# Sums of a layer norm and of a doubly applied norm folded on VectorE, in a two-block transformer kernel

## What is computed

```python
def layernorm(x, g, b):
    mu = jnp.mean(xf, axis=-1, keepdims=True)
    var = jnp.mean(jnp.square(xf - mu), axis=-1, keepdims=True)
    y = (xf - mu) * lax.rsqrt(var + LN_EPS)
    return (y * g + b)

def conformer_conv(h, w_pw1, b_pw1, w_dw, b_dw, ln_g, ln_b, w_pw2, b_pw2):
    u = h @ w_pw1 + b_pw1
    a, gate = jnp.split(u, 2, axis=-1)
    u = a * jax.nn.sigmoid(gate)
    u = depthwise_causal_conv(u, w_dw) + b_dw            # 31 taps
    u = jax.nn.silu(layernorm(u, ln_g, ln_b))
    return u @ w_pw2 + b_pw2

# end of the first block and start of the second: x is normed twice in a row
x = x + sqrelu_mlp(h, ff_w1, ff_w2)                      # second layer: stages up1, down1
x = rmsnorm(x, final_norm_g)                             # out1
h = rmsnorm_2(x, norm_ff1_2)                             # ffa: feeds the gate/up product gu1
```

## Time and profile before

| | |
|---|---|
| median of 3 runs | 1479.2 us (1478.4 to 1481.55) |
| time of the profiled execution | 1481.04 us |
| its span (first to last instruction) | 1478.9 us |
| busy TensorE (PE) / VectorE (DVE) / ScalarE (ACT) | 98% / 74% / 46% of the span |
| granted TensorE clock, mean | 0.998 of full speed |
| LN beside memk1 and memv1, pw2 begins | 148 to 197.3 us |
| down1 | about 778 to 867 us |

### The profile page before, as it was taken

One profiled execution on the slowest core, in us unless ns is written; L12 is line 12 of the kernel. 1 busy time (PEld: TensorE's weight loads), 2 busy tenths in 40 slices (PEclk: granted clock), 3 DMA queues, 4 the chain that ended last, 5 costly groups with the idle time before them and its releaser, 6 DMA issues.

```text
span 1478.9 us, 21797 instructions
## 1 busy us (share of the span) xinstructions
PE 1446.7 (98%) x8556; PEld 1261.6 (85%) x8556; DVE 1092.1 (74%) x1638; ACT 682.5 (46%) x891; POOL 31.5 (2%) x20
## 2 busy tenths in 40 slices
PE   7999999999999999999999999999999999999997
PEld 6878888888889777888888998878888889888887
DVE  3799457688867756557887769998678768788654
ACT  2222254455434554545554345544454356555542
POOL 0000000000000000000000000000005200000000
PEclk9999999999999999999999999999999999999999
DMA  8544444355686433534557747767754445476452
GB/s 316 195 171 150 153 138 158 114 171 202 233 289 218 153 127 128 171 115 143 199 196 270 253 178 259 287 227 240 249 197 154 143 134 188 171 253 217 151 176 68
DMA packets 60192, 279.31 MB, mean 189 GB/s; under 512 B 6633, under 2 KB 8106, under 8 KB 35275
## 3 DMA queue, kind: packets, MB, share of 16 engines
q1 hardware_dynamic: 55672, 266.49, 52.0%
q10 hardware_dynamic: 4434, 11.64, 2.2%
HBM read 273.89 MB, written 4.19 MB: 188 GB/s over the span
## 4 chain that ended last, share of the span: by engine, by line
PE 84%; DVE 8%; DMA 5%; ACT 2%; issue 1%; DVEq 0%; SPq 0%; ACTq 0%
PE acc L474 33%; PE acc L476 17%; PE acc L495 10%; DMA ada_w<-in_ada 5%; PE acc L513 3%; PE acc L514 3%; PE acc L515 3%; DVE wsplit L1650 3%; PE acc L613 2%; PE stat L698 2%; DVE ada_w L2021 2%; PE stat L808 2%; PE score L770 2%; PE acc L617 1%; PE turned L716 1%
## 5 line engine op out<-in xcount | busy, mean ns | idle before, releaser
L474 PE MATMUL acc<-hA,wsplit 128*128 128x512 f32 x1664 | 590.6, 399 | 6.4 <-DVE tsum L1664 4.8
L476 PE MATMUL acc<-hA,wsplit 128*128 128x256 f32 x1664 | 463.9, 279 | 0.0
L1112 ACT ACTIVATE wsplit<-raw 128x2048 fp32r<-128x2048 f32 (+3 forms) x206 | 365.8, 1777 | 191.5 <-PE acc L476 147.0
L1650 DVE TENSOR_TENSOR wsplit<-raw,wsplit 128x2048 fp32r<-128x2048 f32 (+3 forms) x206 | 436.9, 2123 | 7.5 <-ACT wsplit L1112 7.4
L474 PEld LDWEIGHTS acc<-hA,wsplit 128*128 128x128 f32 x1664 | 312.3, 188 | 84.9 <-DVE tsum L1664 5.9
L476 PEld LDWEIGHTS acc<-hA,wsplit 128*128 128x128 f32 x1664 | 313.3, 188 | 0.4
L474 PE MATMUL acc<-hid,wsplit 128*128 128x512 f32 x648 | 225.5, 391 | 1.6 <-issue 1.6
L476 PE MATMUL acc<-hid,wsplit 128*128 128x256 f32 x648 | 182.7, 282 | 0.0
L1122 ACT ACTIVATE lowp<-acc 128x512 f32<-128x512 f32 (+1 forms) x118 | 69.0, 585 | 188.5 <-PE acc L476 164.4
L474 PEld LDWEIGHTS acc<-hid,wsplit 128*128 128x128 f32 x648 | 121.7, 188 | 27.5 <-issue 1.9
L476 PEld LDWEIGHTS acc<-hid,wsplit 128*128 128x128 f32 x648 | 122.5, 189 | 0.1
(11 more groups left out here) (294 smaller groups left out, 2083.7 us busy)
## 6 DMA issues: line engine op xcount, KB each, us to landing
raw<-in_gu SPq DMA_DIRECT2D x44, 1024.0 KB, 5.0
ada_w<-in_ada SPq DMA_DIRECT2D x144, 256.0 KB, 4.7
raw<-in_up SPq DMA_DIRECT2D x32, 1024.0 KB, 4.9
raw<-in_down SPq DMA_DIRECT2D x32, 1024.0 KB, 5.0
raw<-in_dn SPq DMA_DIRECT2D x32, 704.0 KB, 4.3
raw<-in_pw SPq DMA_DIRECT2D x8, 1024.0 KB, 6.4
raw<-in_memk SPq DMA_DIRECT2D x8, 1024.0 KB, 4.9
raw<-in_memv SPq DMA_DIRECT2D x8, 1024.0 KB, 5.3
```

Of the source, the lines that this page charges most:

```text
L474: nc.tensor.matmul(dst.rearrange("p (s t) -> p s t", s=2), w, h, start=start, stop=False, skip_group_check=True)
L476: return nc.tensor.matmul(dst[:, 0:T], lo_w, h[:, 0, :], start=False, stop=stop, skip_group_check=True)
L1112: nc.scalar.activation(wsplit[:, slot, 0, 0:elems_of(n)], raw[:, slot, 0:elems_of(n)], ACT.Copy).then_inc(S("w_hi"), 1)
L1650: V.tensor_tensor(wsplit[:, slot, 1, 0:e], src, wsplit[:, slot, 0, 0:e].bitcast(F32), ALU.subtract).then_inc(S("w_lo"), 1)
```

## The change

The eight tiles of the convolution and the eight tiles of squares of LN are each added up on VectorE to two tiles (three additions of 128x512 for the mean, three for the squares), and TensorE sums each result with two products in place of eight. All four squares are made after chunk 2 of memk1, the inverse root after chunk 3, and the activation goes in three parts behind chunks 0, 1 and 2 of memv1. `ffa` is added to FOLDED; since it has two sums, VectorE also multiplies the squares with their gains and adds them into `lowp` (`weigh`).

```diff
-FOLDED = ["fox", "mixn", "ffb", "final2"]
+FOLDED = ["fox", "ffa", "mixn", "ffb", "final2"]
+LN_MEAN, LN_SQUARES = 3, 6
@@ TensorE, norm_sums
-                            mm = nc.tensor.matmul(stat[:, 1, :], gain_sq[:, 2 * p + j, :], aux[:, p % 2, j, :],
+                            weights = ones[:] if p == first else gain_sq[:, 2 * p + j, :]
+                            squares = lowp[:, j, :] if p == first else aux[:, at, j, :]
+                            mm = nc.tensor.matmul(stat[:, 1, :], weights, squares,
@@ TensorE, LN
             def ln_mean():
                 stat_read(norm_index("mem") + 1)
-                for kt in range(KT):
-                    pe.wait_ge(S("conv_tile"), kt + 1)
-                    mm = nc.tensor.matmul(stat[:, 0, :], ones[:], conv[:, kt, :], start=kt == 0, stop=kt == KT - 1)
+                ln_sum(LN_MEAN)
+
+            def ln_sum(folds):
+                pe.wait_ge(S("ln_folded"), folds)
+                for j in range(2):
+                    mm = nc.tensor.matmul(stat[:, 0, :], ones[:], tsum[:, 0, j, :], start=j == 0, stop=j == 1)
                 mm.then_inc(S("ln_stat"), 1)
-            def ln_squares(pairs):      # eight products over four pairs: gone
...
-                   after=lambda c: ln_mean() if c == 2 else ln_squares([0, 1]) if c == 3 else None)
-            native("memv1", mem_h[1], after=lambda c: ln_squares([2, 3]) if c == 0 else None)
+                   after=lambda c: ln_mean() if c == 2 else ln_sum(LN_SQUARES) if c == 3 else None)
+            native("memv1", mem_h[1])
@@ ScalarE
                     if p >= 2:
-                        wait("ln_stat", p)
+                        wait("ln_folded", LN_MEAN + 1)
...
-                (0, 2): lambda: ln_squares([0, 1]),
-                (0, 3): lambda: ln_squares([2, 3]),
-                (1, 0): ln_root,
-                (1, 1): ln_silu,
-                (1, 2): lambda: None,
+                (0, 2): lambda: ln_squares(range(PAIRS)),
+                (0, 3): ln_root,
+                (1, 0): lambda: ln_silu([0, 1]),
+                (1, 1): lambda: ln_silu([2]),
+                (1, 2): lambda: ln_silu([3]),
@@ VectorE, stage down1
+                def weigh(p):
+                    wait("gain_sq", 2)
+                    for q in range(0 if p == 1 else p, p + 1):
+                        if q >= 1:
+                            wait("weighted", q)
+                        for j in range(2):
+                            squares, weight = aux[:, q % 2, j, :], gain_sq[:, 2 * q + j, 0:1]
+                            if q == 0:
+                                last = V.tensor_scalar(lowp[:, j, :], squares, weight, None, ALU.mult)
+                            else:
+                                last = V.scalar_tensor_tensor(out=lowp[:, j, :], in0=squares, scalar=weight,
+                                                              in1=lowp[:, j, :], op0=ALU.mult, op1=ALU.add)
+                        last.then_inc(S("weighted"), 1)
+                    wait("weighted", p + 1)
...
+                        if norm_name == "ffa":
+                            weigh(p)
                         V.tensor_tensor(aux[:, 1, :, :], aux[:, 1, :, :], aux[:, 0, :, :],
                                         ALU.add).then_inc(S("squares_folded"), 1)
@@ VectorE, LN
             conv_taps(KT * TAPS, KT)
+            def ln_fold(into, first, second, done):
+                V.tensor_tensor(tsum[:, into, :, :], first, second, ALU.add).then_inc(S("ln_folded"), 1)
+                wait("ln_folded", done)
+            wait("conv_tile", KT)
+            ln_fold(0, conv[:, 0:2, :], conv[:, 2:4, :], 1)
+            ln_fold(1, conv[:, 4:6, :], conv[:, 6:8, :], 2)
+            ln_fold(0, tsum[:, 0, :, :], tsum[:, 1, :, :], LN_MEAN)
             for n in range(AHEAD):
                 split_lo(STAGE["pw2"], n, n)
-            wait("conv_tile", KT)
             wait("ln_stat", 1)
...
                 V.tensor_tensor(c2, c2, spread(mu[:], 2), ALU.subtract).then_inc(S("ln_centred"), 1)
+            wait("ln_sq", 2)
+            ln_fold(0, aux[:, 0, :, :], aux[:, 1, :, :], LN_MEAN + 1)
+            wait("ln_sq", PAIRS)
+            ln_fold(1, aux[:, 0, :, :], aux[:, 1, :, :], LN_MEAN + 2)
+            ln_fold(0, tsum[:, 0, :, :], tsum[:, 1, :, :], LN_SQUARES)
             split_lo(STAGE["pw2"], AHEAD, AHEAD)
```

More of the change, by code:

```diff
@@ L688, in norm_sums @@
                         stat_read(q)
-                    if name == "ffa" and p == 0:
+                    if name == "ffa" and p == first:
                         pe.wait_ge(S("gain_sq"), 2)
@@ L864, in ln_mean @@
                 stat_read(norm_index("mem") + 1)
-                for kt in range(KT):
-                    pe.wait_ge(S("conv_tile"), kt + 1)
-                    mm = nc.tensor.matmul(stat[:, 0, :], ones[:], conv[:, kt, :], start=kt == 0, stop=kt == KT - 1)
-                mm.then_inc(S("ln_stat"), 1)
-            def ln_squares(pairs):
[L871 to L876, removed]
+                ln_sum(LN_MEAN)
[3 more added lines that the diff above has]
+                    mm = nc.tensor.matmul(stat[:, 0, :], ones[:], tsum[:, 0, j, :], start=j == 0, stop=j == 1)
+                mm.then_inc(S("ln_stat"), 1)
             native("memk0", mem_h[0], {kt: (S("mem_h"), kt + 1) for kt in range(KT)}, after=relative_biases)
@@ L1461, in ln_root @@
                 wait("log_table", LN_TABLE)
-                wait("ln_stat", 1 + PAIRS)
+                wait("ln_stat", 2)
                 inverse_root("ln_root", 0, stat[:, 0, :], rstd[:], 1 / D, col("ln_eps"))
@@ L1467, in ln_hi, with ln_silu @@
                 nc.scalar.activation(hM[:, 2 * p:2 * p + 2, 0:T], tsum[:, p % 2, :, :], ACT.Copy).then_inc(S("ln_hi"), 1)
-            def ln_silu():
-                for p in range(PAIRS):
+            def ln_silu(pairs):
+                for p in pairs:
                     wait("ln_y", p + 1)
@@ L1484, in ln_silu @@
                         ln_hi(p - 1)
-                ln_hi(PAIRS - 1)
+                    if p == LAST:
+                        ln_hi(p)
             def ln_table():
```

## The result

The changed kernel takes 1468.33 us (1465.84 to 1471.14) against 1479.2 us, both medians of five runs, a ratio of 0.9924 with an interval of 0.9904 to 0.9943. Its profiled execution took 1467.61 us, with a span of 1465.8. In two more comparisons the ratio was 0.9938 [0.9914, 0.9963] and 0.9926 [0.991, 0.9943], so the gain is 9 to 11 us.

A forecast was written before the change was run, and what follows sets the result against it. TensorE, busy 98% of the span, was taken as the bound, with down1's loop of ada loads and reductions right behind. Gains of 4.65 and 0.9 us, 5.55 in all, took 1479.2 to 1473.7 us; range 1470.5 to 1478.6.

The forecast's parts named there:

- Part 1: Layer norm: 5.2 us of products and 1.67 us idle removed, a 2.2 us wait added; pw2 starts 4.65 us earlier.
- The new wait of TensorE: Layer norm, before memv1: TensorE waits 2.2 us, until 164.1, for VectorE's folds of the squares.
- Rival E: Layer norm: TensorE's wait for the squares' folds exceeds 2.2 us and gives back the 4.65; 1479 us, chance 0.04.
- Part 2: ffa's fold in down1: TensorE saves 3.46 us, but only half of VectorE's 1.75 us of waits arrives, 0.9 us.
- This loop of load and reduction: down1: VectorE's ada loads and reductions run about as slowly as TensorE's chunks, the next bound; last tile ends at 867.24.
- The sum: Whole kernel: layer norm's 4.65 plus ffa's 0.9 make 5.55 us, giving 1473.7 us; chance 0.62.
- A: down1: the ada loop speeds up with TensorE, all 3.46 us arrive; total gain 8.1, 1471.1 us, chance 0.12.
- B: down1: VectorE's added work lies on the ada loop in full, -3.9 us; total gain 0.75, 1478.4 us, chance 0.09.
- C: New TensorE gaps before memv1 and ending down1 drop the granted clock; one fall costs 2.85 us, 1476.5 us, chance 0.08.
- its second gap: End of down1: TensorE idles about 2.5 us behind its filler products.
- D: down1: late raw loads meet ada loads, 7.5 for 4.8 us, 2.7 us each; slower, two give 1483.9 us, chance 0.05.
- The estimate of 2.7 us: down1: the page's landing time for a 256 KB ada load, against the row's 4.8 us; spoke for 3.46 us arriving.

The follow-up runs named there:

- e13: Kernel before with 24 instead of 40 products without use ahead of gu2; ratio 1.0002 to the kernel before.
- e15: Kernel before with the layer norm's change alone, ffa summed as before, second look; 1475.44 us, ratio 0.9959.
- e5: Kernel before with 24 instead of 40 products without use ahead of the stage behind down0; ratio 0.9991 to the kernel before.
- e1: Kernel before with the layer norm's change alone, ffa summed as before, first look; 1473.84 us, ratio 0.9963.
- e11: Kernel before, unchanged, measured again; 1481.28 us, ratio to itself 1.0004.
- e6: Changed kernel with 24 instead of 40 products without use ahead of the stage behind down0; ratio 0.9942 to the kernel before.
- e14: Changed kernel with 24 instead of 40 products without use ahead of gu2; ratio 0.9913 to the kernel before.
- e16: Kernel before with the fold of ffa alone, old layer norm kept, second look; 1476.5 us, ratio 0.9972.
- e10: Changed kernel with each ada load cut to 64 of 512 columns and the condition vector scaled by 0.1; 1466.0 us, ratio 0.9901.
- e8: Changed kernel with five more unused additions of 128x512 on VectorE in down1; 1472.38 us, ratio 0.9944.
- e3: Kernel before, unchanged, measured once more; 1479.63 us, ratio to itself 1.0003.

## Why the prediction was right and wrong

**Part 1, right.** 4.65 us forecast, 4.9 us in every profiled execution in which the clock stayed up behind the gap and the activation was in three parts. The new wait of TensorE was 1.93 for 2.2 us, its second sum started at 163.48 for 164.1, hM was ready at 190.6 for 190.9, pw2 started at 191.9 for 192.6 (0.4 us of each is the earlier start). Rival E is out. The steps that gave this are TensorE's count of instructions, and a walk along VectorE's queue, which found the two places where the gain would be cut short.

**Part 2, the mechanism right, the size too small.** Forecast 0.9 us between ends of -3.9 and +3.46, measured 1.7 to 3.5 in all ten executions with the fold and without extra work. The added work took 3.9 us for 4.0, and the waits for `ada_w` took it up. (The lower end is loosely worked out: 4.0 us less the first wait's 1.11 are 2.9, not 3.9.) The step that failed is the sentence "What can bring this forward is only what VectorE waited for TensorE: 1.11 + 0.64 = 1.75 us", of which half was taken, and behind it "This loop of load and reduction runs about as slowly as TensorE's chunks". The rule itself holds: in the changed kernel's profile these waits are gone and the stretch is 1.85 us shorter. But 1.75 us is the number of one execution. All waits of VectorE for TensorE ahead of adds to x in down1, the last one included, were 1.7, 3.3, 5.2 and 3.8 us in the four profiled executions of the kernel before, and 3.7 to 7.5 us in e13, e15, e5 and e1, whose down1 is the same and takes the same 183.0 us. The profile that I read had the least of all eight. In e1 one of these waits stands ahead of the last add (timeline of e1):

```profile
861.98 0.42 DVE L1751 TENSOR_TENSOR x<-x,acc 128x256 f32<-128x256 f32 x1 [3.73 <-PE acc L517]
```

In e5 it was 2.16 us, in e15 1.52, in e11 1.33, in e13 0.34, in the other three none. So the loop ends 0 to 3.7 us ahead of TensorE, depending on how the loads landed, and a wait that is nearly as long as its cover in a single profile doesn't say that both end together each time. The term should have been 1.75 us in full at least, with 3.46 as its upper end.

**The sum, a term left out.** This step of the prediction weighs most in the miss. "4.65 + 0.9 = 5.55 us" passes the gain of the two places on to the end and puts all that lies behind ffa at nothing, without a reason given. In the profiled executions the stages behind it gave 5.4 us: 2.0 in gu1, 1.0 in dn1, 2.4 in gu2 with dn2. Part 2 was 1.1 us too small, part 1 0.2. gu1's 2.0 us go with the fold of ffa, as shown above; some 0.35 us of them are the first product of gu1, 3.67 us behind the variance instead of 4.02. Of dn1's 1.0 us, 0.9 are falls of the clock. gu2's are mostly its rhythm. In the timed runs less is left for these stages, since the whole gain is 9 to 11 us there: some 2 to 4 us.

**Rivals.** A's 3.46 us came in full in e6, e14 and e16 (and with short loads in e10), but in none of the four executions of the changed kernel itself; elsewhere it was 1.7 to 2.9 us. B is out: neither the 3.9 us of the change nor the 3.6 us more of e8 lay on the path in full. C is real but rare behind the first gap: one fall in eleven profiled executions, and 1.7 us instead of 2.85. The clock was low for less time than I took from the start of the run: 0.67, 0.50, 0.50 and 0.63 in four windows of one us. At its second gap, forecast at 2.5 us and 1.1 us long at most, the clock stayed up. What C missed is that the kernel before has such waits too. In one profile none was above 1.7 us, in others they reached 2.28 us in dn1, with falls. The Trainium skill (TensorE: Matmul & The Clock Gate, HAM oscillation) says that waits between bursts can put the array back to half rate. The traces agree in kind, with 0.50 behind waits of 1.85 to 2.78 us in seven executions and 1.00 behind waits of 1.93 to 2.05 us in twelve places. D did not appear: down1's worst landing after was 6.5 us.

**Page against row.** The landings after have a median of 5.0 us in down1, and even an eighth of the bytes took 3.7 and 3.8 us, so the rows were the right price. The estimate of 2.7 us, worked out from the Trainium skill (DMA: Bandwidth & Descriptors, Latency and other measured facts; Where 436 GB/s comes from), was the median of no run. That rival A, for which it spoke, came in some runs all the same has another reason, the loop's slack.

**The range.** Its lower end, 1470.5, was A with next to no allowance for stages that the change leaves alone. With 4.9 and even the full 3.5 us the time would have been 1470.8, inside it; with the 2.0 us of down1 in the table, 1472.3. What lies beyond comes from gu1, dn1 and gu2, whose lengths I had taken as fixed. The profile had a hint that I passed over: in gu1 the chain of waits is on VectorE and the ada loads, so whatever moves their landings moves the end. In single executions of the same kernel before, gu1 with dn1 varied by 3.0 us, and gu2 with dn2 by 2.9.

What stays open: by what way the fold of ffa shortens gu1 beyond the 0.35 us of its first product (the ada tiles come earlier there, but no run separates cause and effect); what sets the rhythm in gu2; when a wait of some 2 us brings the clock down; and why the profiled executions differ by 12.8 us (1478.6 and 1465.8, means of four spans) where all timed ones say 9 to 11, of which the falls of the clock in e3 and e11 explain 0.9.

## What to carry to other kernels

When a saving on the first bound is cut off by a second one that ends just behind it, look at what the second one waited for: waits for loads shrink and grow with the work beside them and hid 3.9 us of added work here, so the second bound is a range and not a point. One profile gives one point of it: read the same waits in several executions of the unchanged kernel before forecasting, and look there at the granted clock too. Give stages whose chain of waits lies on loads a term and a width of their own in the sum, changed code or not. Moving work earlier on a queue (the activation, 1.9 us) can be worth as much as removing it.

## What the hardware showed that was not expected

- One stream of products has two rhythms at full granted clock, 346.7 and 353.3 ns a pair, and can stay in one for tens of us. The stages up0, down0, up1, down1, dn1 and dn2 were at 346.7 or 346.8 in nearly all executions (347.1 at most); only gu1, gu2 and the mixers' stages showed the slower one.
- Behind a gap of 1.95 us ahead of memv1 TensorE was once at half clock (0.50 in two windows of one us, 0.67 and 0.63 beside them), behind a gap of 1.93 us at the same place it wasn't. In dn1 the same happened at waits of 1.85, 2.04, 2.13, 2.28, 2.39 and 2.78 us in six executions, and not at 2.05 us in a seventh. e15 had one fall beside the attention fox, at 498 us, with no wait of TensorE above 0.9 us near it. Each fall cost some 1.7 us.
- A load of 32 KB in place of 256 KB landed after 3.7 to 3.8 us in place of 4.8 to 5.0 (medians in down1), beside loads of 1 MB on the same queue.
